# Inverting the key triangle of a gated DeltaNet: levels as products of 128 rows by 32 columns, and the sample state's outer products after the levels

## The reference

```python
decay = jnp.exp(jnp.where(incl, G[..., :, None] - G[..., None, :], -jnp.inf))
kk = jnp.einsum('nbhid,nbhjd->nbhij', kc, kc)
m = jnp.where(strict, bc[..., :, None] * kk * decay, 0.0)
a_mat = m + jnp.eye(CHUNK, dtype=m.dtype)
rhs = jnp.concatenate([vc * bc[..., None], kc * (bc * jnp.exp(G))[..., None]], axis=-1)
sol = lax.linalg.triangular_solve(a_mat, rhs, left_side=True, lower=True, unit_diagonal=True)
...
s = s * jnp.exp(g_t)[..., None, None]
u = b_t[..., None] * (v_t - jnp.einsum('bhk,bhkv->bhv', k_t, s))
s = s + jnp.einsum('bhk,bhv->bhkv', k_t, u)
return s, jnp.einsum('bhk,bhkv->bhv', q_t, s)
```

## Time and profile before

| | |
|---|---|
| median of three runs | 1552.25 us (1550.82 to 1553.25) |
| the profiled execution | 1555.09 us, of which the span from first to last instruction is 1553.3 us |
| PE busy | 1501.0 us (97% of the span), 15959 matmul records |
| DVE, ACT, POOL busy | 526.1, 350.2, 83.5 us |
| mean granted TensorE clock | 0.977 |

### The profile page before, as it was taken

One profiled execution on the slowest core, in us unless ns is written; L12 is line 12 of the kernel. 1 busy time (PEld: TensorE's weight loads), 2 busy tenths in 40 slices (PEclk: granted clock), 3 DMA queues, 4 the chain that ended last, 5 costly groups with the idle time before them and its releaser, 6 DMA issues.

```text
span 1553.3 us, 35786 instructions
## 1 busy us (share of the span) xinstructions
PE 1501.0 (97%) x15959; PEld 879.8 (57%) x15959; DVE 526.1 (34%) x870; ACT 350.2 (23%) x601; POOL 83.5 (5%) x136
## 2 busy tenths in 40 slices
PE   9999977879999999999999999999999999999998
PEld 8989875679999998943333333333333333333332
DVE  6767833366666568430110111101101101111104
ACT  6565532344444444320000000000000000000001
POOL 0011112200000000010000000000000000000010
PEclk9999997699999999999999999999999999999999
DMA  6778630345554575799999999999999999999993
GB/s 262 290 272 278 212 120 4 134 137 190 182 173 173 169 289 218 296 415 403 419 399 419 419 401 420 419 400 420 413 407 420 401 419 420 400 420 419 418 419 155
DMA packets 78064, 490.89 MB, mean 316 GB/s; under 512 B 9305, under 2 KB 9561, under 8 KB 53217
## 3 DMA queue, kind: packets, MB, share of 16 engines
q1 hardware_dynamic: 70000, 460.45, 74.8%
q0 software_dynamic: 7920, 28.25, 5.2%
HBM read 464.74 MB, written 23.92 MB: 315 GB/s over the span
## 4 chain that ended last, share of the span: by engine, by line
PE 89%; DVE 4%; ACT 3%; issue 2%; DMA 1%; SPq 0%; DVEq 0%; ACTq 0%
PE PP L2461 37%; PE PP L1836 23%; PE PP L2471 19%; DVE dlo L382 2%; ACT dhi L376 1%; PE PP L2072 1%; DMA ring<-in_mkv 1%; PE PP L2139 1%; PE PP L2061 1%; PE PP L1954 0%; PE PP L1938 0%; PE PP L2344 0%; PE PP L1930 0%; PE PP L1916 0%; PE PP L2171 0%
## 5 line engine op out<-in xcount | busy, mean ns | idle before, releaser
L2461 PE MATMUL PP<-ring,gen 128*32 128x448 f32 x6144 | 578.8, 539 | 1.2 <-DVE gen L1690 1.2
L2461 PEld LDWEIGHTS PP<-ring,gen 128*32 128x32 f32 x6144 | 199.6, 110 | 379.6 <-issue 377.9
L2471 PE MATMUL PP<-ring,gen 128*32 128x512 f32 x2688 | 289.9, 592 | 0.0
L1836 PE MATMUL PP<-uh,dhi 128*128 128x264 f32 x736 | 214.0, 291 | 2.8 <-DVE dlo L382 1.9
L1836 PE MATMUL PP<-ul,dhi 128*128 128x264 f32 x736 | 209.6, 285 | 0.0
L1836 PE MATMUL PP<-uh,dlo 128*128 128x264 f32 x736 | 209.3, 284 | 0.0
L382 DVE TENSOR_TENSOR dlo<-ring,dhi 128x2048 fp32r<-128x2048 f32 (+2 forms) x85 | 175.5, 2065 | 93.6 <-ACT dhi L376 93.3
L1774 DVE TENSOR_TENSOR gen<-ubuf,PP 128x448 f32<-128x448 f32 x48 | 26.9, 617 | 516.6 <-PE PP L2461 516.6
L2471 PEld LDWEIGHTS PP<-ring,gen 128*32 128x32 f32 x2688 | 87.3, 110 | 199.9 <-issue 199.9
L1028 ACT ACTIVATE ubuf<-PP 128x448 f32<-128x448 f32 x48 | 22.6, 544 | 780.2 <-PE PP L2461 780.2
L376 ACT ACTIVATE dhi<-ring 128x2048 fp32r<-128x2048 f32 (+2 forms) x85 | 147.1, 1730 | 107.7 <-PE PP L1836 81.3
(11 more groups left out here) (473 smaller groups left out, 1361.4 us busy)
## 6 DMA issues: line engine op xcount, KB each, us to landing
ring<-in_w_up SPq DMA_DIRECT2D x256, 896.0 KB, 21.1
ring<-in_w_down SPq DMA_DIRECT2D x112, 1024.0 KB, 21.9
ring<-in_wi SPq DMA_DIRECT2D x22, 1024.0 KB, 4.8
ring<-in_a_in SPq DMA_DIRECT2D x18, 1024.0 KB, 7.4
ring<-in_wo SPq DMA_DIRECT2D x16, 704.0 KB, 4.1
slot_rows<-ring POOLq DMA_DIRECT2D x25, 384.0 KB, 5.0
ring<-in_mkv SPq DMA_DIRECT2D x8, 1024.0 KB, 4.9
ring<-in_kc SPq DMA_DIRECT2D x8, 1024.0 KB, 8.9
```

The costliest lines, as they stand in the source:

```text
L1836: mm = pe.matmul(out, lhs[l], rhs[r], start=first and i == 0, stop=last and i == 2)
L2461: mm = pe.matmul(bank((c // KD % 2) * SG + g)[SL * q:SL * (q + 1), 0:FQ], xs[:, at_:at_ + SL], w[:, q * FQ:(q + 1) * FQ], start=(k == 0), ...
L2471: return pe.matmul(out[SL * quarter:SL * (quarter + 1), :], hT[:, at_:at_ + SL], w[:, k * D + h * 512:k * D + (h + 1) * 512], start=(j == ...
```

## The change

Each level's blocks are laid out as a block diagonal over all 128 rows, so that one matmul per head takes the place of four blocks: the stationary operand has 128 rows and 32 columns, the moving one 128 by 128. That takes a write of the block diagonals at every step. `diagonal(lv, c)` copies the inverse into `Ub[c]`: POOL quadrants 0 and 1, ACT quadrant 2, DVE quadrant 3. `y_blocks` copies the first product out of PSUM into `Yw[c]`: ACT quadrants 0 and 1, DVE 2 and 3. The level masks are applied once for all levels, in `masked(c)` (DVE, 1,024 columns), and the transpose of the inverse is made by PE (`turn`, against the identity) and copied out by ACT (`turned`, into `UC[c]`). `new_blocks` now subtracts 256 columns; at the last level a transpose on DVE follows. `ON_ACT` and `ON_DVE` count the steps on the semaphores.

The rest moves with it. `sample_columns` and the blocks of `kq_diag` go from DVE to POOL; the scaling of the queries for chunk 1 (`qd`) goes on POOL ahead of the levels; `key_rows(1)` comes first and `key_rows(0)`, `sample_rows` and `triangle(1)` behind the levels. No outer product stands between the level steps any more: `outer(0)` to `outer(3)` stand between the products with the values, and 4 to 7 in a row ahead of `head_sums`. ACT's `faded(0)` comes after the half blocks, and `urow` behind it.

```diff
-            def step_rows_(lv, c):
+            def diagonal(lv, c):
+                v.wait_ge(s("dl_tu"), 2 * lv + c + 1)
+                v.tensor_copy(heads128(Ub[c])[quad(3), :, quad(3)], heads32(TU[c][:, 0:HALF])[quad(3)]).then_inc(s("dl_ym"), 1)
+
+            def masked(c):
+                if c:
+                    v.wait_ge(s("ain_mm"), 36)
+                v.tensor_tensor(steps[c].rearrange("p (l x j) -> p l x j", l=LV - 1, j=32),
+                                heads32(bank(4 - 2 * c)[:, 0:HALF]).unsqueeze(1).to_broadcast([P, LV - 1, H, 32]),
+                                step32.unsqueeze(2).to_broadcast([P, LV - 1, H, 32]), ALU.mult).then_inc(s("dl_ym"), 1)
+
+            def y_blocks(lv, c):
                 v.wait_ge(s("dl_y"), 2 * (lv - 1) + c + 1)
-                v.tensor_tensor(heads32(Y32[c]), heads32(bank(5 - 2 * c)[:, 0:HALF]), step32[lv].unsqueeze(1).to_broadcast([P, H, 32]),
-                                ALU.mult).then_inc(s("dl_ym"), 1)
+                for b in range(2, 4):
+                    ins_ = v.tensor_copy(heads128(Yw[c])[quad(b), :, quad(b)], heads32(bank(5 - 2 * c)[:, 0:HALF])[quad(b)])
+                ins_.then_inc(s("dl_ym"), 1)
...
             def step_y(lv, c):
-                pe.wait_ge(s("dl_tu"), 2 * (lv - 1) + c + 1)
-                blocks32(bank(5 - 2 * c)[:, 0:HALF], key_block(c), block_of(TU[c])).then_inc(s("dl_y"), 1)
+                spread_in(lv - 1, c)
+                if lv == 1:
+                    pe.wait_ge(s("dl_ym"), ON_DVE["masked", 0, c])
+                for x in range(H):
+                    at_ = (lv - 1) * HALF + 32 * x
+                    mm = pe.matmul(bank(5 - 2 * c)[quad(x % 4), x // 4 * P:x // 4 * P + P], steps[c][:, at_:at_ + 32], Ub[c][:, head(x)],
+                                   start=True, stop=True)
+                mm.then_inc(s("dl_y"), 1)
...
+            def turn(lv, c):
+                pe.wait_ge(s("dl_tu"), 2 * lv + c + 1)
+                if lv == 0:
+                    pe.wait_ge(s("dl_ym"), ON_DVE["masked", 0, c])
+                for x in range(H):
+                    at_ = HALF + x // 4 * P
+                    mm = pe.matmul(bank(4 - 2 * c)[quad(x % 4), at_:at_ + P], TU[c][:, 32 * x:32 * x + 32], ident, start=True, stop=True)
+                mm.then_inc(s("dl_tr"), 1)
```

More of the change, by code:

```diff
@@ new lines, in _ @@
+            pool.wait_ge(s("dl_ud"), 1)
+            diagonal(0, 0)
+            diagonal(0, 1)
+            pool.wait_ge(s("dl_ud"), 3)
+            sample_columns()
+            pool.wait_ge(s("sd_in"), 1)
+            diagonal(1, 0)
+            pool.wait_ge(s("dl_ud"), 4)
+            sample_blocks()
+            pool.wait_ge(s("sd_in"), 2)
+            diagonal(1, 1)
+            for lv in range(2, LV - 1):
+                for c in range(2):
+                    diagonal(lv, c)
+            for c in range(2):
+                pool.wait_ge(s("dl_tu"), 2 * (LV - 1) + c + 1)
+                for b in range(2):
+                    ins_ = pool.tensor_copy(heads128(Ub[c])[quad(b), :, quad(b)], heads32(TU[c][:, HALF:2 * HALF])[quad(b)])
+                ins_.then_inc(s("dl_ud"), 1)
@@ L902, in _ @@
             solved(0)
+            faded(2)
             a.wait_ge(s("dl_tok"), 5)
@@ L1447, in _ @@
             v.tensor_copy(Sb, PP[2][:, :]).then_inc(s("S_done"), 1)
-            state_sum(7)
+            for k in range(3, 8):
+                state_sum(k)
             cat_low(H, H + XH, slice(0, T))
@@ L2057, in grow, with gram @@
                 mm.then_inc(s("dl_grow"), 1)
-            def gram(c, m1, out):
-                for x in range(H):
+            def gram(c, m1, out, heads=range(H)):
+                for x in heads:
                     mm = pe.matmul(out[:, head(x)], act[:, 8 + x, cols(c)], act[:, m1 + x, cols(c)], start=True, stop=True)
-                mm.then_inc(s("dl_kk"), 1)
+                if H - 1 in heads:
+                    mm.then_inc(s("dl_kk"), 1)
             def tokens(c, m0, out):
@@ new lines, in _, with sample_sums @@
+            step_z(1, 1)
+            step_y(2, 0)
+            turn(1, 1)
+            pe.wait_ge(s("dl_vt"), 3)
+            pe.wait_ge(s("dl_kt"), 1)
+            gram(0, 0, PP[0], range(4))
+            step_z(2, 0)
+            step_y(2, 1)
+            turn(2, 0)
+            gram(0, 0, PP[0], range(4, H))
+            step_z(2, 1)
+            step_y(3, 0)
+            turn(2, 1)
+            def sample_sums(n0, n1):
+                for n in range(n0, n1):
+                    g = n % 4
+                    mm = pe.matmul(bank(6)[32 * g:32 * g + 32, 0:P], kq_diag[:, 32 * n:32 * (n + 1)], state[:, n * P:(n + 1) * P],
+                                   start=(n < 4), stop=(n >= DBH - 4))
+                return mm
@@ L2207, in _ @@
+            tokens(0, 8, PP[0])
             pair_z(0)
             pair_z(1)
+            pe.wait_ge(s("sd_u"), 1)
+            pe.transpose(bank(6)[:, P:2 * P], upad, ident).then_inc(s("sd_rows"), 1)
             half_y(0)
             half_y(1)
-            outer(5)
+            pe.wait_ge(s("dl_kt"), 2)
+            gram(1, 0, PP[0])
             half_z(0)
```

335 lines of the change are left out of this document (192 added, 143 removed).

## The result

The changed kernel takes 1535.15 us, the median of five executions (1534.51 to 1542.62), against 1553.25 us (1550.82 to 1554.01) for the kernel before on the same chip. The ratio is 0.9902 with a 95% interval of 0.9876 to 0.9928: faster, by 18 us between the medians, where 27 were forecast. The profiled execution took 1535.07 us, its span 1533.5.

The account below looks back on a forecast made before the run. PE was taken as the bound except in the DeltaNet stage, whose levels were bound by PE's instruction count; -30.2 - 13.7 + 13.1 + 0.6 + 3 = -27.2 us against 1552.25 gave 1525.0 us, range 1517 to 1538.

Parts of the forecast that it names:

- The stalls of A: Levels, 62.8 us before: PE runs out of instructions every 128 records (256 instructions), 18.0 us of it outright.
- Rival 2: Levels: the stalls are not instruction fetch and come back at each wait, +18 us, 1543; chance 0.04.
- A, 24.9 + 7.7: Levels: 24.9 us of PE work plus 7.7 of added waits, 32.6 instead of 62.8 us, -30.2.
- The transpose on DVE: End of the levels: no profile row, put between 0.3 and 0.85 us, taken as 0.42.
- rival 4: Levels: POOL is the bound, copies taking 0.8 instead of 0.41 us cost 3 to 6 us, 1530; 0.80 together with the forecast.
- B, 11.5: 64- and 128-blocks: outer products and 7.9 us of waits leave, 11.5 against 25.2 us, -13.7.
- C, 32.3: Products with the values, up to head_sums: eight outer products instead of two, 32.3 against 19.2 us, +13.1.
- Both waits: Products with the values: PE waits 2.7 us for Sb, and 2.3 for ACT's copy and squares behind the last outer product.
- the step of the ladder: Last outer products before head_sums: outer 1.13 + sums 1.27 + 0.15 = 2.55 us each.
- D, 21.9 + 0.6: Norms and first tiles, 21.9 us before: DVE reaches the reciprocal 0.6 us later than PE's sums, +0.6.
- I allow 3 us: Clock term: the last four outer products leave PE 45% busy for 8 us, so the norms' products start slow, +3.
- Rival 1: Half clock in the value products alone, 1544, or in the 64- and 128-blocks and the value products' last half, 1541; chance 0.10.

## Why the prediction was right or wrong

**The stalls of A: right.** "128 records are 256 instructions" holds in every gap between stalls; the stalls are gone, ten packets instead of nineteen, and they come back with small products alone. Rival 2 falls.

**A, 24.9 + 7.7: right to 0.3 us,** with small errors that cancel. PE was busy 25.72. The transpose on DVE, bounded by 0.3 and 0.85, is 0.45. POOL's copies of two quadrants take 0.82 to 0.95, the longest while DVE copies its own, and PE never waits for POOL, so rival 4 did not come; `sample_blocks` is 1.25 for eight copies and 0.29 for each of two more, inside its bounds.

**B, 11.5: the sum is 12.55 at full clock,** 1.0 too low, and 17.45 as it ran. That PE waits some 2 us for `upad` was right.

**C, 32.3: 33.2 at full clock,** 0.9 too low, and 36.65 as it ran. Both waits and the step of the ladder were as forecast.

**D, 21.9 + 0.6: 22.22** at a clock of 0.77, near the 0.84 of before; 21.38 where the clock is 1.00 throughout, and 24.27 as it ran.

**The step that failed is the clock's term, "I allow 3 us".** The clock cost at least 10.4 us: 4.9 in B, 3.4 in C, 2.1 in D. I placed the loss in the ladder and D alone. Rival 1, half clock in B and the last half of C, which I gave one chance in ten, is what happened in kind, if at about half of its price: it was put at 8 + 11 us, for all of B and half of C, and the clock fell behind B's start, came back at its end, and took a smaller part of C. What spoke for it stood in the earlier trace rows, B at 0.50 throughout, and I did not ask why. The waits for `state_sum` in B were not needed for it: without them, in the kernel with the outer products moved alone, B is at 0.50 as well. The sum did not look at how B is entered. The end of the levels, where I counted the exposed waits one by one (0.5, 1.1, 0.9, the transposes), is the very place where PE is busy for about half the time, and the earlier trace rows showed that the clock falls after such a slice. With the waits there and in B filled, B ran at 1.00 in 12.55 us; with only B's own large wait gone it stayed at 0.57. No run fills the end of the levels alone, so how much of B's clock hangs on that place by itself is open.

Without the clock the sum is 2.0 us too low (98.9 against 100.87); with the 3 us allowed and the 10.4 paid it is 9.4 too low. The time of 1535.15 us lies in the range, 3 us below its upper end; the gain is two thirds of the one forecast, and 2 us of it are the stage's earlier start, which the change did not make.

## What to carry to other kernels

Count instructions, not only busy time: where an engine's tiny matmuls wait for nothing that the profile can name, at a regular number of records, wider tiles give the time back even when each does four times the arithmetic. When a change thins PE's work just ahead of a long stretch, price the stretch at both clocks, and look for a wait ahead of it that independent work can fill: here products that nothing reads gave some 10 us. The same instructions in another order, with no extra work, gave 13 us on top of the change's 18 to 20, part of it the clock and the larger part the ladder and the two waits that went. Work moved out from under a bound is free only where something covers it again: outer products in a row, each waiting for the sums before it, cost 2.6 to 3.5 us apiece, and 1.1 between other products.

## What was not expected of the hardware

Half clock lasted while PE was fully busy, and for very different times. In the kernel with the spread outer products PE had no wait from 244.8 us on, and the clock stayed at 0.50 until about 264.6:

```profile
246.00:248.00 2.00, 2.00 (x21) 2.00 (x21) 0.39 (x1) 0.59 (x1) 0.00 (x0) 0.50 0.00 0
...
262.00:264.00 2.00, 2.00 (x10) 2.00 (x11) 1.22 (x2) 0.85 (x3) 2.00 (x4) 0.50 0.00 0
264.00:266.00 2.00, 2.00 (x12) 1.31 (x11) 0.00 (x0) 0.76 (x2) 1.77 (x4) 0.85 0.00 0
```

In the changed kernel, with the same instructions on PE up to the first product with the values, full clock was back at about 250.9 us, 6.8 us after PE's last wait. And the kernel with all the products that nothing reads has 120 more records in the stage than the changed one (1,340 against 1,220, summed over the four rows) and is the fastest.
